# A dense feed-forward in two phases, its products by a seven-product scheme

## The reference

```python
def swiglu(t, w1, w3, w2):
    return (jax.nn.silu(t @ w1) * (t @ w3)) @ w2
# layer 0: t is (256, 1024); w1, w3 are (1024, 2816); w2 is (2816, 1024), all float32
# then x = layer_norm(ALPHA * t + swiglu(t, w1, w3, w2))
```

## Time and profile before

| | us |
|---|---|
| median of three runs | 1797.5 (1797.35 to 1797.84) |
| the profiled execution | 1794.48 |
| its span | 1792.7 |
| TensorE busy in it | 1720.6 |
| VectorE, ScalarE busy in it | 727.2, 368.4 |

### The profile page before, as it was taken

How to read it: one execution, slowest core, us unless ns; L and a number is a source line. 1 busy time by engine, 2 the same in 40 slices (tenths; PEclk the granted TensorE clock), 3 DMA queues, 4 the chain that set the end, 5 groups by cost and what they waited for, 6 DMA issues and landing times.

```text
span 1792.7 us, 64698 instructions
## 1 busy us (share of the span) xinstructions
PE 1720.6 (96%) x29278; PEld 1511.8 (84%) x29278; DVE 727.2 (41%) x1816; ACT 368.4 (21%) x858; POOL 2.9 (0%) x12
## 2 busy tenths in 40 slices
PE   7999999999999899999999999999999999989987
PEld 6878878677777787887858999999999999989986
DVE  6976745201110497674543222322223222222324
ACT  5443422101000644342212000000000000000001
POOL 0000000000000000000000000000000000000000
PEclk9999999999999999999999999999999999999999
DMA  8333223524434433322367999999999999999995
GB/s 312 112 116 110 103 73 129 188 106 154 162 140 140 154 112 100 118 96 73 131 280 295 425 426 426 426 426 427 425 426 427 426 424 399 404 376 427 425 426 214
DMA packets 55111, 473.28 MB, mean 264 GB/s; under 512 B 5280, under 2 KB 5568, under 8 KB 20960
## 3 DMA queue, kind: packets, MB, share of 16 engines
q1 hardware_dynamic: 53456, 463.49, 64.3%
q10 hardware_dynamic: 1184, 5.75, 0.9%
q0 software_dynamic: 368, 2.64, 0.4%
HBM read 470.80 MB, written 1.06 MB: 263 GB/s over the span
## 4 chain that ended last, share of the span: by engine, by line
PE 76%; DMA 16%; DVE 4%; issue 2%; ACT 1%; SPq 0%; DVEq 0%; ACTq 0%
PE bank L1120 18%; DMA ring<-in_moe 15%; PE bank L885 11%; PE bank L1040 10%; PE bank L539 9%; PE bank L942 8%; PE bank L962 4%; PE bank L902 3%; PE bank L924 3%; PE bank L1067 2%; PE bank L1110 1%; PE bank L665 1%; PE bank L713 1%; PE bank L796 1%; PE bank L492 1%
## 5 line engine op out<-in xcount | busy, mean ns | idle before, releaser
L1120 PE MATMUL bank<-arena,ring 128*64 128x80 f32 (+2 forms) x8192 | 306.4, 232 | 17.7 <-DMA ring<-in_moe 10.7
L1120 PEld LDWEIGHTS bank<-arena,ring 128*64 128x64 f32 x8192 | 290.7, 137 | 24.8 <-issue 13.5
L2102 DVE TENSOR_TENSOR arena<-arena,bank 128x80 f32<-128x80 f32 (+2 forms) x224 | 52.9, 236 | 513.0 <-ACT arena L1419 513.0
L1419 ACT ACTIVATE arena<-bank 128x80 f32<-128x80 f32 (+3 forms) x246 | 61.5, 250 | 893.7 <-PE bank L1120 705.3
L885 PE MATMUL bank<-xT,ring 128*128 128x256 f32 x1024 | 227.7, 381 | 4.8 <-DVE arena L1732 4.8
L1120 PE MATMUL bank<-arena 128*64 128x80 f32 (+2 forms) x6144 | 224.8, 233 | 3.3 <-issue 2.1
L885 PEld LDWEIGHTS bank<-xT,ring 128*128 128x128 f32 x1024 | 192.8, 190 | 34.7 <-issue 8.9
L1120 PEld LDWEIGHTS bank<-arena 128*64 128x64 f32 x6144 | 216.4, 138 | 5.9 <-issue 3.3
L1040 PE MATMUL bank<-arena,ring 128*64 128x80 f32 (+2 forms) x4096 | 163.7, 232 | 3.7 <-issue 3.7
L539 PE MATMUL bank<-xT,ring 128*128 128x256 f32 x704 | 157.2, 385 | 7.8 <-DMA ring<-in_w_in 7.8
L1040 PEld LDWEIGHTS bank<-arena,ring 128*64 128x64 f32 x4096 | 153.8, 137 | 8.1 <-issue 4.1
(11 more groups left out here) (414 smaller groups left out, 1488.8 us busy)
## 6 DMA issues: line engine op xcount, KB each, us to landing
ring<-in_moe SPq DMA_DIRECT2D x128, 1536.0 KB, 15.8
arena<-in_moe SPq DMA_DIRECT2D x96, 1536.0 KB, 14.6
ring<-in_ffn SPq DMA_DIRECT2D x22, 1536.0 KB, 6.5
ring<-in_w_gate SPq DMA_DIRECT2D x32, 1024.0 KB, 4.9
ring<-in_w_in SPq DMA_DIRECT2D x14, 1536.0 KB, 6.7
ring<-in_w_branch SPq DMA_DIRECT2D x8, 1024.0 KB, 4.9
ring<-in_w_out SPq DMA_DIRECT2D x8, 1024.0 KB, 6.6
arena<-ml_rows ACTq DMA_DIRECT2D x4, 512.0 KB, 4.8
```

The costliest lines, as they stand in the source:

```text
L1120: last = mm(bank[c:c + STRIP, g * CAP:g * CAP + n], w[:, at:at + STRIP], rhs[:, kt, 0:n], start=(kt == 0), stop=(kt == KT - 1), skip_group ...
L1419: f(ff_sl[:, i % 2, 0:n], bank[:, 0:n], ACT.Silu).then_inc(S["h_silu"], 1)
L2102: tt_(ACTIVE_H[:, i, 0:PLACES[e]], ff_sl[:, s % 2, 0:PLACES[e]], bank[:, CAP:CAP + PLACES[e]], ALU.mult)\
```

## The change

The dense part is cut into two phases. First all 22 gate and up blocks are computed and the whole hidden activation, 22 blocks, stays on chip (`h_all`). Then the down products run over eleven pairs of hidden blocks.

Units 2 to 21 of the first phase compute one 2x2 block product: the two rows are gate and up, the two columns are the token halves, and the contraction is cut in two halves of 512. Such a product takes eight block products in the plain form; the new one takes seven (the Winograd form), each of four 128x128x128 products, and needs sums of blocks first and sums of results afterwards. VectorE makes the sums of the weights (`up_sums`, four of 128x512 per unit), of the activations (`x_sums`, once) and of the results (`up_mixed`). ScalarE copies the first result out of its bank. The seven results of one unit are 128x128 each and lie in three banks; two sets of three banks take turns.

In the second phase the contraction halves are the two hidden blocks of a pair, the rows are the token halves, the columns the halves of the model width. VectorE makes four sums of the hidden blocks and four of the weights per pair (`down_sums`). Each of the seven products is summed over all eleven pairs in a bank of its own, and the seven are put together once, at the end, on VectorE (`down_mix`, called inside `norm`). Five residual starts, each of one bank, replace four.

The preparation of layer 1's tables moves behind pairs 0, 2, 4 and 6 on VectorE and behind the first phase on ScalarE. The weights come in 22 units of 1 MB and then 11 of 1 MB. The loops of TensorE and SyncE over the units are written out.

```diff
-        S5_TABLES_AT, S5_WEIGHTS_AT = (4, 7, 12), 16
+        S5_TABLES_AT, S5_WEIGHTS_AT = (0, 2, 4), 6
+        UP_BANKS = ((0, 1, 4), (2, 3, 5))
+        DOWN_BANK = {"P1": 0, "P2": 4, "P3": 6, "P4": 5, "P5": 7, "P6": 1, "P7": 2}
+        DOWN_FIRST = ("P1", "P2", "P4", "P5", "P6", "P3", "P7")
+        DOWN_LAST = ("P1", "P2", "P6", "P5", "P3", "P7", "P4")
...
+            def hidden(n):
+                w = unit_wait(pe, ("ff", n))[:, 0, :]
+                a, b, first = (banks[k] for k in UP_BANKS[n % 2])
+                if n >= 4:
+                    pe.wait_ge(S["up_freed"], n - 3)
+                def product(out, left, right):
+                    for k in range(4):
+                        last = mm(out, left[:, k * P:(k + 1) * P], right[:, k, :], start=(k == 0), stop=(k == 3))
+                    return last
...
+                inc(product(at(first, 0), quarter(0, 0), x(0, 0)), "up_first")
+                product(at(a, 0), quarter(0, 1), x(1, 0))
+                pe.wait_ge(S["x_sums"], 1)
+                product(at(b, 0), quarter(1, 1), x_sum[:, 3])
+                pe.wait_ge(S["up_sums"], n - 1)
+                product(at(b, 1), sums[:, 0], x_sum[:, 0])
+                product(at(a, 1), sums[:, 1], x_sum[:, 1])
+                product(at(b, 2), sums[:, 2], x_sum[:, 2])
+                inc(product(at(a, 2), sums[:, 3], x(1, 1)), "h_filled")
...
+            def down(p):
+                w = unit_wait(pe, ("down", p))
...
+                for k, name in enumerate(DOWN_LAST if end else DOWN_FIRST):
+                    if k == 2:
+                        pe.wait_ge(S["dn_sums"], p + 1)
...
+                    left, right = sides[name]
+                    last = mm(banks[DOWN_BANK[name]][:, :], left, right,
+                              start=(p == 0 and name in ("P1", "P6", "P7")), stop=end, skip_group_check=True)
+                    if end:
+                        inc(last, "dn_part")
...
 ScalarE:
+                for n in range(2, FF_STEPS):
+                    act.wait_ge(S["up_first"], n - 1)
+                    act.wait_ge(S["up_freed"], n - 2)
+                    step(nc.scalar.copy(up_mix[:, 7, :], banks[UP_BANKS[n % 2][2]][:, 0:P]), "up_copied", hold=False)
+                    act.wait_ge(S["gate_summed"], n - 1)
+                    act.wait_ge(S["h_ready"], n - 1)
+                    f(ff_sl[:, n % 2, :], flat(up_mix[:, 0:2, :]), ACT.Silu).then_inc(S["h_silu"], 1)
...
 VectorE:
+            def up_sums(n):
...
+                step(tt_(s_(2), a11, a21, ALU.subtract), hold=False)
+                step(tt_(s_(0), a21, a22, ALU.add))
+                step(tt_(s_(1), s_(0), a11, ALU.subtract))
+                step(tt_(s_(3), a12, s_(1), ALU.subtract), "up_sums", hold=False)
+            def down_sums(p):
...
+                step(tt_(t(2), b22, b12, ALU.subtract), hold=False)
+                step(tt_(s_(2), a11, a21, ALU.subtract), hold=False)
+                step(tt_(s_(0), a21, a22, ALU.add), hold=False)
+                step(tt_(t(0), b12, b11, ALU.subtract))
+                step(tt_(s_(1), s_(0), a11, ALU.subtract), hold=False)
+                step(tt_(t(1), b22, t(0), ALU.subtract))
+                step(tt_(s_(3), a12, s_(1), ALU.subtract), hold=False)
+                step(tt_(t(3), b21, t(1), ALU.subtract), "dn_sums", hold=False)
+            def up_mixed(n):
+                dve.wait_ge(S["h_filled"], n + 1)
...
+                step(tt_(up_mix[:, 0:3:2, :], bc(up_mix[:, 7, :], 1, 2), pair(a, 0), ALU.add))
+                step(tt_(up_mix[:, 3:5, :], bc(up_mix[:, 2, :], 1, 2), pair(b, 1), ALU.add))
+                step(tt_(up_mix[:, 1, :], up_mix[:, 3, :], part(a, 2), ALU.add), "gate_summed", hold=False)
+                step(tt_(up_mix[:, 5:7, :], bc(up_mix[:, 4, :], 1, 2), pair(b, 0), ALU.add), "up_freed", hold=False)
...
             def dense():
...
+                for n in range(2, FF_STEPS):
+                    up_mixed(n)
+                    if n + 2 < FF_STEPS:
+                        up_sums(n + 2)
+                    else:
+                        dve.wait_ge(S["h_ready"], 2 * (n + 3 - FF_STEPS))
+                        down_sums(n + 2 - FF_STEPS)
...
+                for p in range(FF_PAIRS):
+                    if p + 2 < FF_PAIRS:
+                        dve.wait_ge(*down_done(p))
+                        down_sums(p + 2)
...
+                    if p in S5_TABLES_AT:
+                        s5_tables(1, S5_TABLES_AT.index(p))
+            def down_mix(k):
...
+                if k == 0:
+                    dve.wait_ge(S["dn_copied"], 1)
+                    dve.wait_ge(S["dn_part"], 2)
+                    step(tt_(c(0), p1, P_("P2"), ALU.add), hold=False)
+                    dve.wait_ge(S["dn_part"], 3)
+                    step(tt_(u2, p1, P_("P6"), ALU.add))
+                if k == 1:
+                    dve.wait_ge(S["dn_part"], 4)
+                    step(tt_(u4, u2, P_("P5"), ALU.add))
+                    dve.wait_ge(S["dn_part"], 5)
+                    step(tt_(c(1), u4, P_("P3"), ALU.add))
+                if k == 2:
+                    dve.wait_ge(S["dn_part"], 6)
+                    step(tt_(u3, u2, P_("P7"), ALU.add))
+                    dve.wait_ge(S["dn_part"], 7)
+                    step(tt_(c(2), u3, P_("P4"), ALU.add), hold=False)
+                    step(tt_(c(3), u3, P_("P5"), ALU.add))
```

More of the change, by code:

```diff
@@ L511, in route_first, with residual @@
                     fill(last, ("logits",))
-            def residual(bank, tt, hf, doubled):
+            def residual(bank, tt, hf, kind, first=True):
                 for q in range(4):
@@ L935, in all_banks_free @@
                     pe.wait_ge(S[jobs[n][0]], jobs[n][1])
[L937 to L944, removed]
-            def dense():
[L948 to L967, removed]
-                all_banks_free()
[L970 to L978, removed]
@@ new lines, in dense @@
+            def dense():
+                assert len(jobs) % RB == 0 and first_ff[0] % RING == 0
+                all_banks_free()
+                for n in range(2, FF_STEPS):
+                    hidden(n)
+                    if n == 3:
+                        pe.wait_ge(S["h_ready"], 2)
+                        residual(banks[DOWN_BANK["P3"]], 0, 1, 0)
+                        residual(banks[DOWN_BANK["P3"]], 1, 1, 2, first=False)
+                        residual(banks[DOWN_BANK["P5"]], 1, 1, 0)
+                pe.wait_ge(S["up_copied"], FF_STEPS - 2)
+                residual(banks[DOWN_BANK["P2"]], 0, 0, 0)
+                residual(banks[DOWN_BANK["P4"]], 1, 0, 0)
+                for p in range(FF_PAIRS):
+                    down(p)
@@ L1421, in dense @@
             def dense():
[L1422 to L1430, removed]
+                for n in range(2):
+                    gate_hidden(n, n, T, banks[6 + n], first=True)
+                for n in range(2, FF_STEPS):
[5 more added lines that the diff above has]
+                    f(ff_sl[:, n % 2, :], flat(up_mix[:, 0:2, :]), ACT.Silu).then_inc(S["h_silu"], 1)
+                act.wait_ge(S["pv2_loaded"], 16)
+                s5_tables(1, 0)
+                s5_tables(1, 1)
+                act.wait_ge(S["dn_part"], 1)
+                step(nc.scalar.copy(dn_mix[3], banks[DOWN_BANK["P1"]][:, :]), "dn_copied", hold=False)
             def experts():
@@ L1964, in norm, with x_sums @@
                                     ALU.mult), name, hold=False)
[L1966 to L1972, removed]
-            def dense():
[L1975 to L1979, removed]
+            def x_sums():
+                b11, b12, b21, b22 = (xT[:, 4 * half:4 * half + 4, tt * P:(tt + 1) * P] for half in range(2)
+                                      for tt in range(2))
+                t = lambda k: x_sum[:, k]
+                dve.wait_ge(S["xT_ready"], 4)
+                dve.wait_ge(S["xT_ready_dve"], 2)
+                step(tt_(t(2), b22, b12, ALU.subtract), hold=False)
+                step(tt_(t(0), b12, b11, ALU.subtract))
+                step(tt_(t(1), b22, t(0), ALU.subtract))
+                step(tt_(t(3), b21, t(1), ALU.subtract), "x_sums", hold=False)
```

115 lines of the change are left out of this document (86 added, 29 removed).

## The result

The changed kernel takes 1774.6 us (median of 4 runs, 1772.2 to 1776.6) against 1797.4 (4 runs, 1796.0 to 1797.8). The ratio is 0.9879, 95% interval 0.9866 to 0.9893. Two later measurements of the same two kernels gave 0.9890 (0.9874 to 0.9906) and 0.9887 (0.9870 to 0.9903): 19.9 and 20.1 us by the medians, where the first gave 22.8. The forecast was 1779.2, range 1774 to 1786.

A forecast was written before the change was run, and what follows sets the result against it. The prediction took the dense feed-forward to be bound by TensorE alone. Its terms, -13.1 - 9.4 + 0.9 + 0.7 + 2.2 + 0.4 = -18.3, turned 1797.5 into 1779.2 us, range 1774 to 1786.

The forecast's parts named there:

- Bound by TensorE alone, and the gain passes through whole: Dense feed-forward, 365.3 to 582.7 us: TensorE busy 217.40 of 217.40 us; later work waits for its result.
- The rival without gain: Experts' stretch: its transfers set the end and do not start earlier, 1797 us; chance 0.02.
- Gate and up, -13.1: First phase: 56 instructions of 128 columns replace 32 of 256, 6.25 us for 6.91, over 20 units -13.1 us.
- The rival of the loads: Up phase: 128-column instructions run at the weight load's 192 ns, not 112, so slower, 1869 us; chance 0.03.
- Down, -9.4: Second phase: 14 instructions of 512 columns a pair instead of 16, 6.01 us for 6.87, over 11 pairs -9.4 us.
- Residual starts, +0.9: Residual starts of the down sums: five in place of four, 0.91 us each, +0.9 us.
- Late sums, +0.7: Down phase: layer 1's tables queued on VectorE ahead of sums that TensorE wants, total lateness +0.7 us.
- The rival in which every step is waited for: Down phase: VectorE decides, lateness at its upper bound 4.2 us, +3.5 on the forecast, 1782.7 us; chance 0.11.
- VectorE in the up phase, 4.6 to 4.7 against 6.25: First phase: VectorE's sums, mixing and product take 4.6 to 4.7 us a unit beside TensorE's 6.25; cost 0.
- Loads, ScalarE, change of phase, each 0: Weight loads, ScalarE's added copy in the up phase, and the passage from up to down each cost 0.
- The end, +2.2 and +0.4 by the clock: After the last pair: VectorE's chain delays normalised values, +2.2 us; first transposes at the lower clock, +0.4 us.
- Long low clock: Behind the pause at the end: 48 next products stay at 1.2 GHz, 4.8 us more, 1784.0 us; chance 0.10.

The follow-up runs named there:

- up scheme alone: Changed kernel with the down products put back to their plain form, eight per pair: 1783.1 us, ratio 0.9936 to the kernel before.
- down scheme alone: Changed kernel with the gate and up products put back to plain ones of 256 columns: 1789.4 us, ratio 0.9969 to the kernel before.

## Why the prediction was right

The step numbers are those of the prediction, in its order, against the trace after.

- *Bound by TensorE alone, and the gain passes through whole*: right. -18.4 in the stretch, and the experts' stretch keeps its length, 848.9 and 849.8. The rival without gain is out. Outside the stretch C to D is shorter too, which no term foresaw (below).
- *Gate and up, -13.1*: -12.9 with this scheme alone. 6.25 us a unit, as forecast. The weight loads stay covered also where VectorE writes the weights in the same time: 192 ns each (the median of all groups of L961) in a pitch of 112, and TensorE has no idle time before the groups of L961 shown. The rival of the loads is out.
- *Down, -9.4*: 154 instructions at 0.429 are 66.1; from 493.07 to 559.99 there are 66.9, of which 0.7 are late sums; -9.4 for the products holds.
- *Residual starts, +0.9*: three take 2.8 us (375.64 to 378.42) and two 1.9, 4.7 against 3.65, +1.0.
- *Late sums, +0.7*: late starts of 0.43 and 0.08 at pairs 5 and 9, none at 7, are 0.5 where 0.7 of lateness was forecast; 0.1 twice in the instructions behind them, which I had not counted, makes it 0.7. Cutting the tables gave 0.7 back. So the mechanism is right, and that the size is right to a tenth is luck. The rival in which every step is waited for is out. (The second part of the tables is 6.84 us by the earlier trace rows, not 6.87; it changes nothing.)
- *VectorE in the up phase, 4.6 to 4.7 against 6.25*: 4.5 from the start of the mixing to the end of the product. Hidden, and two more sums fit where four do not.
- *Loads, ScalarE, change of phase, each 0*: right. Besides the late sums, the list of TensorE's waits from 363 to 563 us is empty.
- *The end, +2.2 and +0.4 by the clock*: from the end of TensorE's last pitch to the first values 2.73 us, and 0.66 before (its last 16 instructions start at 575.82 and take 16 x 0.429, to 582.68; the values start at 583.34), +2.1. The +0.4 for the clock did not come: B to C became shorter, 14.2 to 14.6 in place of 14.8 to 15.1. One part of that is plain: the normalised values now come from on-chip memory instead of a bank, two in 1.00 us against 1.53, which I had not counted.
- *Long low clock*: out. The 16 instructions behind the pause take 3.75 us as before, and the 48 later ones 5.36 (5.66 before).
- *A sign that did not fit its own terms*: "about 199 us" to the last down product. The terms give 217.3 - 13.1 - 9.4 + 0.9 + 0.7 = 196.4, and the trace has 559.99 - 363.05 = 196.9. It is the first normalised value that comes after 199.7.

Sum against the profiled execution: forecast -18.3, measured 1776.6 - 1794.5 = -17.9. The terms that lie in the dense stretch add up to -18.7, and it gave -18.4: that is the mechanism. That the whole of the profiled execution agrees as well is luck, because the other stretches moved by -2.2, -0.9, -2.3, +5.0 and +0.9 us and happen to cancel to +0.5.

The median fell by more: 22.8, 19.9 and 20.1. The forecast for it, 1779.2, is 4.6 us too high, and the measured 1774.6 lies only 0.6 above the lower end of the range. I had added the whole 3.0 us between the profiled run and the median of before; such a distance is a matter of the run, and after it was 2.0 us the other way. 3.0 + 2.0, less the 0.4 of the sum above, is the 4.6.

C to D is 302.7 twice in the kernel before, 300.4 to 301.1 in four traces (the changed kernel three times, the up scheme alone), and 302.1 to 302.3 in the other six. Two things make it up. The first are waits of TensorE for nothing that the profile shows. In the kernel before there are (columns: waiter, us in total, times, longest):

```profile
PE bank L703 <- issue: 1.4, 2, 1.0
...
PE bank L665 <- issue: 1.2, 1, 1.2
```

and in the changed kernel (L718 is the same code as L703) only:

```profile
PE bank L718 <- issue: 0.7, 2, 0.4
```

These are 1.9 of the 2.3 us. They go with the kernels: 2.6 us in both traces of the kernel before and 2.2 with the down scheme alone, 0.7 to 1.0 in all nine traces with the up scheme. The second thing is the clock behind a pause. The 32 instructions of the gate there, first in the changed kernel, then in the one with two more sums:

```profile
761.17 7.15 PE L900 MATMUL bank<-xT,ring 128*128 128x256 f32 x32 [2.39 <-DVE arena L1778]
```

```profile
763.26 8.83 PE L900 MATMUL bank<-xT,ring 128*128 128x256 f32 x32 [2.40 <-DVE arena L1778]
```

They take 8.83 us in all five kernels with an edit of the sums, the tables or the mixing, and 7.14 or 7.15 in the other seven traces, behind the same pause of 2.4 us. 300.4 + 1.7 = 302.1: those five have the short waits and pay for the clock, the down scheme alone has the long waits and does not pay. So the 2.3 us of this stretch are not made by less work in it. The short waits came with every kernel that has the up scheme, and they are about what the medians show beyond 18.4. Why the waits and the clock there depend on code elsewhere stays open, and with it whether another kernel would keep the 2 us.

## What to carry to other kernels

A seven-product scheme pays on an engine that is bound by products as long as the sums fit beside them: compare the second engine's cycle per unit with the new, shorter cycle of the first, not with the old one. Look also at what else is in its queue: a block of small work that is longer than the slack up to the next sums is paid in waits (here 6.8 us with 2.5 us of slack a pair). Cut the traces of two kernels at the same events before explaining a difference of their times: here the stretch with the change repeated within 0.05 us, while the others moved by up to 5 us with the same instructions in them. Take the same trace of the unchanged kernel twice: only that showed that the low clock at the router is not the change's. The work put together at the end of such a scheme is on the path; put first what the next stage needs first, on each engine that the next stage passes through.

## What the runs showed of the hardware that I had not expected

- Behind one and the same pause TensorE can run at the low or at the full clock. At the router (a pause of 1.35 us) the unchanged kernel took 1.97 us for 32 instructions in one execution and 3.51 in another; over all kernels the stretch varies by 5 us (42.7 to 47.8). In layer 1's mixers (a pause of 2.4 us) 32 instructions take 7.15 or 8.83 us.
- VectorE writes two 128x512 normalised blocks in 1.00 us from on-chip memory and in 1.53 us from a bank.
- Pauses of TensorE of 0.4 to 1.2 us that nothing in the profile releases, 2.6 us in total before and 0.7 after, in a part that the change does not touch.
- A late start of TensorE costs a little more than the wait: the six instructions behind a late start took 2.84 us, and 2.74 elsewhere.
